# More landing places for the experts' value rows, in columns of the activations that are already used

## The chip, the cores and the metric

The kernel runs on one core of a Trainium2 chip. The metric is the device time of one execution in microseconds (us); the median of three runs stands for it.

## The reference, cut to what matters

One inference step of a two-layer decoder for 256 prompt tokens and 32 sample tokens (288 in all, width 1024). Each layer has an attention or state-space mixer and then a PEER channel mixer. In PEER, each token picks 16 experts for each of 8 heads out of 128 x 128 = 16384 experts:

```python
q = (xc @ w_q).reshape(P_CHUNK, P_HEADS, 2, P_DKEY // 2)
...
g = jax.nn.softmax(sc.astype(F32), axis=-1)
act = jax.nn.gelu(jnp.einsum('td,thkd->thk', xc, u_tab[eid]).astype(F32))
return jnp.einsum('thk,thkd->td', g * act, v_tab[eid].astype(F32)).astype(h.dtype)
```

So each token needs 128 rows of `v_tab`, each of 1024 float32 (4 KB), weighted by gate times activation and summed. For 288 tokens and two layers these are 576 sets of 128 rows, 512 KB each.

## The kernel before, in words

`peer(l)` stands once for each engine. TensorE first computes the activations of **all** experts for all tokens (`hidden`, lines 860 to 862): 128 steps, and ScalarE writes each step's result into `HID`, an SBUF region of four blocks (`HB[0]` to `HB[3]`, 9216 floats a partition each). A block is laid out column by column: 32 floats for each token, prompt tile 0 first (four tokens of a group side by side, `hidden_column`), then prompt tile 1, then the 32 sample tokens in columns 256 to 287.

Then comes the **value stage**, which the change touches. It goes over 72 groups of four tokens: 8 groups of sample tokens, then 32 groups of prompt tile 0, then 32 of prompt tile 1 (`GROUPS`, `NGR` = 72). TensorE's program is a loop over q (in `peer` of the tensor engine, after line 962), in a fixed order:

- `spread_i1(q)` (L889) copies the tokens' first expert indices over all partitions; VectorE makes a one-hot matrix of it (`one_hot`, L1974);
- `pick(q-1)` (L900) multiplies the one-hot matrix with the tokens' columns of `HID`: this is the last reading of these columns in this layer; it raises `picked_full`. VectorE then makes the weights (`weights`, L1981, L1988);
- `values(q-2)` (L918 for sample groups, L923 for prompt groups) multiplies the weights with the four tokens' gathered rows and adds up in PSUM; it waits for the four gathers and raises `v_used`.

The rows come by **gathers**: GpSimd issues one indirect DMA for each token (L639), 288 a layer, in the order of the groups, into `NVS` = 9 slots of 1024 floats (`VS`), used in turn. Gather n uses slot n modulo 9. The first nine wait for the end of the activations (`hidden_full` against `VS_FREE`), since these slots were buffers of that stage; each later one waits until the slot's former content is used: `v_used` >= (n - 9) // 4 + 1. GpSimd's program is in order, so a gather that waits holds up all later ones.

In layer 0 TensorE does work for the next layer inside the same loop: 64 key projections and 16 sets of sums (`key_norms`, L941 and L950), 20 steps in groups 29 to 38 and 60 steps in groups 43 to 71 (`NORM_PLACES`); VectorE and ScalarE do the state-space factors and the keys' squares beside it. These use parts of `HID` whose columns are picked already: pages of the latent cache land in `HB[2]` and `HB[3]` (SyncE loads them, L413, after 24 groups are picked), the factors, turns and key scales lie in `HB[0]` and `HB[1]`. Layer 1 has nothing beside its loop. After group 71 of layer 0 the odd layer begins; after group 71 of layer 1 the result is stored.

The lines that set the gathers' places and waits before:

```python
VS_FREE = [NK - 4 + n + 1 for n in range(4)] + [NK - 1, NK] + 3 * [NK]
...
if n < NVS:
    pool.wait_ge(sem("hidden_full"), l * NK + VS_FREE[n])
else:
    pool.wait_ge(sem("v_used"), l * NGR + (n - NVS) // 4 + 1)
```

Of the kernel before, what the change touches and what calls it, by code (L numbers as in the profile page):

```python
# [19 lines left out]
P = 128  # L20
D = 1024
# [3 lines left out]
NT = SEQ + NS  # L25
# [18 lines left out]
PH, TOPK, NK = 8, 16, 128  # L44
# [81 lines left out]
def build(nc, I, O, stop=4):  # L126
    ctx = ExitStack()
    with ctx:
# [140 lines left out]
        VS = [tile_at(f"v_slot{n}", [D], at) for n, at in enumerate(VS_AT)]  # L269
# [147 lines left out]
        def _(sp):  # L417
# [10 lines left out]
            load(ident, I["ident"], "ident_loaded")  # L428
            load(X[:, 1, :], I["x_prompt"][P:SEQ, :], "x_loaded1")
            load(gain, I["gain"], "gain_loaded")  # L430
# [3 lines left out]
            load(iota, I["iota"], "const_loaded")  # L434
            load(group, I["group"], "const_loaded")
            load(before, I["before"], "const_loaded")
            load(pages, I["page_table"], "pages_loaded")
            for n in range(1, 4):
                load(W_IN0[:, :, 512 * n:512 * n + 512], I["ev_w_in"][:, :, 512 * n:512 * n + 512], f"w_in0_loaded{n}")
            load(GAIN0, I["gain0"].partition_broadcast(P), "gain0_loaded")  # L440
            load(TBL0, I["tbl0"], "tbl0_loaded")
# [21 lines left out]
            load(TBLA, I["tbla"], "tbls_loaded")  # L463
            load(TBLB, I["tblb"], "tbls_loaded")
            load(TBLBN, I["tblbn"], "tbls_loaded")
# [17 lines left out]
            load(W_OUT, I["ev_w_out"], "w_out_loaded")  # L483
# [3 lines left out]
            def peer_loads(l):  # L487
# [17 lines left out]
                if l == 0 and live(3):  # L505

                    sp.wait_ge(sem("picked_full"), NS // 4)
                    load(S5P[:, 0:3, :], I["s5_par"], "s5_par_loaded")
                    load(BBD, I["s5_b"], "s5_b_loaded")
                    load(W_UKN, I["mla_w_uk"], "s5_b_loaded")  # L510
# [11 lines left out]
                    load(W_IN1, I["od_w_in"], "w_in1_loaded")  # L522
# [3 lines left out]
            if live(3):  # L526

                sp.wait_ge(sem("x_updated"), 2)
                load(GROW, I["grow"].partition_broadcast(P), "odd_small_loaded")
                load(GQN, I["mla_g_qn"].partition_broadcast(P), "odd_small_loaded")  # L530
                load(GQR, I["mla_g_qr"].partition_broadcast(P), "odd_small_loaded")
                load(GKN, I["mla_g_kn"].partition_broadcast(P), "odd_small_loaded")
                load(GKNP, I["mla_g_kn_col"], "odd_small_loaded")
                load(COS, I["cos"], "odd_small_loaded")
                load(SIN, I["sin"], "odd_small_loaded")
                load(W_UK, I["mla_w_uk"], "odd_small_loaded")
                load(W_UV, I["mla_w_uv"], "odd_small_loaded")
                load(W_UKT, I["mla_w_ukt"], "odd_small_loaded")
                load(W_GLU, I["s5_w_glu"], "odd_small_loaded")
                load(TBLD, I["tbld"], "odd_small_loaded")  # L540
                load(S0, I["state_c"], "odd_small_loaded")
                load(CBD, I["s5_c"], "odd_small_loaded")
                load(DSKIP, I["s5_d"], "odd_small_loaded")
                load(BGLU, I["s5_b_glu"], "odd_small_loaded")

                sp.wait_ge(sem("h_ready"), 18)
                load(W_UQ, I["mla_w_uq"], "w_uq_loaded")
# [13 lines left out]
                load(TBLDN, I["tbldn"], "tbldn_loaded")  # L561
# [19 lines left out]
                for n in range(2):  # L581
                    load(W_OUT1[n], I["od_w_out"][:, :, 512 * n:512 * n + 512], f"w_out1_loaded{n}")
# [20 lines left out]
        def _(pool):  # L603
# [14 lines left out]
            def peer(l):  # L618
# [11 lines left out]
                n = 0  # L630
                for g in GROUPS:
                    for t in group_tokens(g):
# [6 lines left out]
                        pool.indirect_dma_start(out=VS[n % NVS], out_offset=None, in_=v_rows,  # L639
                                                in_offset=bass.IndirectOffsetOnAxis(ap=IDX[:, at:at + 1], axis=0)).then_inc(sem(f"v_loaded{n % NVS}"), 16)  # L640
                        n += 1
# [27 lines left out]
        def _(pe):  # L669
# [90 lines left out]
            def out_projection(l, OT):  # L760
                pe.wait_ge(sem(f"ot_ready{l}"), 1)
                for n in range(2 if l else 1):
                    pe.wait_ge(sem(f"w_out1_loaded{n}" if l else "w_out_loaded"), 16)
# [32 lines left out]
            def peer(l):  # L796
# [106 lines left out]
                def values(q):  # L903
# [7 lines left out]
                    for i in range(4):  # L911
                        n = 4 * q + i
                        pe.wait_ge(sem(f"v_loaded{n % NVS}"), 16 * (l * (NT // NVS) + n // NVS + 1))
                    if kind == "sample":
                        for i in range(4):
                            w = WZ[:, 4 * (q % 4) + i, 31 - (4 * j + i):63 - (4 * j + i)]
                            for g in range(4):
                                ins = pe.matmul(banks[4][32 * g:32 * g + 32, 0:256], w, VS[(4 * q + i) % NVS][:, 256 * g:256 * g + 256],  # L918
                                                start=False, stop=False, skip_group_check=True)
# [1674 lines left out]
```

## Time and profile before

| what | us |
|---|---|
| median of 3 runs | 2413.12 (2412.98 to 2414.96) |
| span of the profiled execution, first to last instruction | 2379.3 |
| median less that span | 33.8 |
| gathers of layer 0, first to last issue | 730.5 to about 1168 |
| value groups 9 to 71 of layer 1 | 1989.8 to 2374.7 |
| TensorE busy in the whole span | 2003.3 (84%) |
| GpSimd busy in the whole span | 978.3 (41%) |

No time of its own is given for the profiled execution beyond its span; the 33.8 us between the span and the median lie around the span. In the profile, PE is TensorE, PEld its weight loads, DVE VectorE, ACT ScalarE, POOL GpSimd, SP SyncE; L639 is line 639. "PEclk" or "granted clock" is the share of TensorE's full clock. "DMA share" is the mean busy share of the core's 16 DMA engines; it adds up packet durations, so that overlapping packets can bring it a little over 1.

### The profile page before, as it was taken

The page shows a single profiled execution, that of the slowest core. Times are in us where ns is not written, and L with a number is a line of the kernel's source. Part 1 is how long each engine was busy: PE and PEld are TensorE (multiplying, and loading weights), DVE is VectorE, ACT ScalarE, POOL GpSimd, SP SyncE. Part 2 cuts the span into 40 slices and gives each one's busy share as a digit, 9 for nine tenths or more (in the row PEclk, how much of TensorE's full clock was granted, in tenths as well). Part 3 has the DMA queues.
Part 4 walks back from the last instruction along what each step waited for, and adds up shares of the span by engine and source line. Part 5 has one row for each costly group of instructions (what it writes and reads, how often), then busy time and mean ns, then how long its engine had stood idle before and what let it go on. Part 6 is the DMA issues. An engine that isn't in the chain of part 4 may idle for free.

```text
span 2379.3 us, 38222 instructions
## 1 busy us (share of the span) xinstructions
PE 2003.3 (84%) x14225; PEld 1500.4 (63%) x14225; DVE 1200.7 (50%) x3489; ACT 649.6 (27%) x977; POOL 978.3 (41%) x832
## 2 busy tenths in 40 slices
PE   9878999999998668889798478999999986666666
PEld 4554799999996333334366247999999963233322
DVE  2553499623333433588456944997233333333332
ACT  1331244555552001111124022455555520000000
POOL 0010368850003566666411303588500036655664
PEclk9898999999999789999887699999999998988887
DMA  6454424445457999999922334244545579998998
GB/s 231 188 208 160 151 90 160 160 160 166 163 168 242 345 338 379 373 369 354 344 72 64 88 110 151 86 159 159 165 162 167 165 249 335 357 354 321 349 337 311
DMA packets 176793, 529.89 MB, mean 223 GB/s; under 512 B 22018, under 2 KB 49186, under 8 KB 176098
## 3 DMA queue, kind: packets, MB, share of 16 engines
q0 software_dynamic: 86912, 309.64, 35.9%
q1 hardware_dynamic: 88546, 217.30, 27.0%
q8 instruction: 114, 1.87, 0.3%
q10 hardware_dynamic: 1152, 0.52, 0.1%
q14 instruction: 69, 0.57, 0.1%
HBM read 524.69 MB, written 2.69 MB: 222 GB/s over the span
## 4 chain that ended last, share of the span: by engine, by line
PE 58%; DMA 18%; POOL 9%; DVE 7%; issue 5%; ACT 2%; SPq 0%; POOLq 0%; DVEq 0%; ACTq 0%
DMA v_slot<-in_peer_v,v_rows 16%; PE bank L860 10%; PE bank L862 10%; PE bank L861 10%; PE bank L687 9%; PE bank L923 8%; POOL v_slot L639 6%; POOL u_low L627 3%; PE bank L1001 2%; PE bank L918 1%; PE bank L941 1%; DMA u_slot<-in_peer_ut 1%; PE bank L806 1%; PE bank L900 0%; DMA w_in<-in_od_w_in 0%
## 5 line engine op out<-in xcount | busy, mean ns | idle before, releaser
L639 POOL DMA_INDIRECT v_slot<-in_peer_v,v_rows x576 | 544.7, 946 | 771.5 <-PE bank L862 441.1
L860 PE MATMUL bank<-h_parts,u_high 128*128 128x288 f32 x2048 | 607.0, 296 | 7.4 <-POOL u_low L627 5.8
L861 PE MATMUL bank<-h_parts,u_high 128*128 128x288 f32 x2048 | 604.4, 295 | 0.0
L862 PE MATMUL bank<-h_parts,u_low 128*128 128x288 f32 x2048 | 602.8, 294 | 0.0
L923 PE MATMUL bank<-v_slot,weight_columns 128*32 128x512 f32 x2048 | 304.9, 720 | 208.6 <-DMA v_slot<-in_peer_v,v_rows 205.7
L860 PEld LDWEIGHTS bank<-h_parts,u_high 128*128 128x128 f32 x2048 | 384.1, 188 | 11.2 <-POOL u_low L627 9.2
L862 PEld LDWEIGHTS bank<-h_parts,u_low 128*128 128x128 f32 x2048 | 385.7, 188 | 0.0
L861 PEld LDWEIGHTS bank<-h_parts,u_high 128*128 128x128 f32 x2048 | 384.6, 188 | 0.0
L1429 ACT CAST u_high<-u_slot 128x1024 fp32r<-128x1024 f32 x256 | 268.8, 1050 | 400.1 <-PE bank L862 244.2
L627 POOL TENSOR_TENSOR u_low<-u_slot,u_high 128x1024 fp32r<-128x1024 f32 x120 | 319.2, 2670 | 95.0 <-ACT u_high L1429 95.0
L1961 DVE TENSOR_TENSOR u_low<-u_slot,u_high 128x1024 fp32r<-128x1024 f32 x136 | 166.7, 1226 | 277.7 <-ACT u_high L1429 277.7
L1974 DVE TENSOR_SCALAR i_one_hot<-bank,keep 128x512 f32<-128x512 f32 x144 | 108.0, 751 | 383.9 <-PE bank L889 377.0
L923 PEld LDWEIGHTS bank<-v_slot,weight_columns 128*32 128x32 f32 x2048 | 69.0, 121 | 346.2 <-issue 300.4
L1981 DVE SCALAR_TENSOR_TENSOR i_one_hot<-keep,i_pairs,bank 128x128 f32<-128x128 f32 x576 | 165.7, 344 | 58.3 <-PE bank L900 58.0
L1459 ACT ACTIVATE hidden_rows<-bank 128x288 f32<-128x288 f32 x256 | 180.9, 707 | 10.4 <-PE bank L862 10.3
L900 PE MATMUL bank<-hidden_rows,i_one_hot 128*128 128x128 f32 x1152 | 174.4, 299 | 3.4 <-DVE i_one_hot L1974 3.4
L900 PEld LDWEIGHTS bank<-hidden_rows,i_one_hot 128*128 128x128 f32 x1152 | 158.4, 210 | 26.0 <-issue 15.8
L622 POOL TENSOR_TENSOR w_q_low<-w_q,w_q_high 128x1024 fp32r<-128x1024 f32 x24 | 57.2, 2393 | 198.8 <-ACT w_q_high L1439 198.8
L889 PEld LDWEIGHTS bank<-i_tokens,keep 128*128 128x128 bf16 x576 | 37.0, 105 | 139.7 <-issue 137.8
L1525 ACT ACTIVATE key_squared<-bank 128x512 f32<-128x512 f32 x64 | 38.2, 597 | 295.7 <-PE bank L941 295.7
L413 POOL DMA_DIRECT2D region<-in_pool_kv x32 | 17.4, 543 | 173.6 <-issue 173.6
L687 PE MATMUL bank<-h_parts,w_q_high 128*128 128x288 f32 x384 | 77.9, 298 | 0.0
(368 smaller groups left out, 2297.9 us busy)
## 6 DMA issues: line engine op xcount, KB each, us to landing
u_slot<-in_peer_ut SPq DMA_DIRECT2D x256, 512.0 KB, 3.5
w_q<-in_peer_w_q SPq DMA_DIRECT2D x8, 2048.0 KB, 17.4
v_slot<-in_peer_v,v_rows POOLq DMA_INDIRECT x576, 6.2
region<-in_cache_a_kt SPq DMA_DIRECT2D x8, 960.0 KB, 11.3
region<-in_cache_a_v SPq DMA_DIRECT2D x8, 960.0 KB, 12.7
region<-in_ev_w_in SPq DMA_DIRECT2D x3, 2048.0 KB, 15.6
region<-in_pool_kv POOLq DMA_DIRECT2D x32, 128.0 KB, 3.3
region<-in_pool_kv SPq DMA_DIRECT2D x32, 128.0 KB, 3.3
```

The source lines that it names most:

```text
L627: pool.tensor_tensor(ULOW[e % 4], US[e % 4], UHIGH[high_slot(e)].bitcast(F32), ALU.subtract).then_inc(sem("u_split_by_pool"), 1)
L639: pool.indirect_dma_start(out=VS[n % NVS], out_offset=None, in_=v_rows, in_offset=bass.IndirectOffsetOnAxis(ap=IDX[:, at:at + 1], axis=0)) ...
L687: ins = pe.matmul(out, lhsT, rhs, start=(n == 0), stop=(n == len(pairs) - 1))
L860: pe.matmul(bank, uh, HR[:, 0, c, :], start=(c == 0), stop=False)
L861: pe.matmul(bank, uh, HR[:, 1, c, :], start=False, stop=False)
L862: ins = pe.matmul(bank, ul, HR[:, 0, c, :], start=False, stop=(c == KC - 1))
L900: ins = pe.matmul(out, OH1[:, q % 2, i, :], HID[:, :, hidden_column(t), :], start=True, stop=True)
L923: ins = pe.matmul(banks[6 - 2 * kind + h][32 * i:32 * i + 32, :], WZ[:, 4 * (q % 4) + i, 31 - j:63 - j], VS[(4 * q + i) % NVS][:, 512 * h: ...
L1429: act.copy(UHIGH[high_slot(e)], US[e % 4]).then_inc(sem("u_high"), 1)
L1459: act.activation(HID[:, e // ROWS, :, e % ROWS], banks[4 + e % 4][:, 0:NT], ACT.Gelu_apprx_tanh).then_inc(sem("gelu_done"), 1)
L1961: dve.tensor_tensor(ULOW[e % 4], US[e % 4], UHIGH[high_slot(e)].bitcast(F32), ALU.subtract).then_inc(sem("u_split_by_dve"), 1)
L1981: step(dve.scalar_tensor_tensor(out=OH1[:, q % 2, i, :], in0=iota, scalar=I2T[:, t:t + 1], in1=banks[2 + q % 2][:, i * P:i * P + P], op0=A ...
```

## The change

Layer 0 gets nine and layer 1 eight further slots of 1024 floats, in columns of `HID` that have been picked. A table, worked out when the program is built, gives each gather its slot, the semaphore and count it waits for, and how many landings its slot has had by then. A slot stands in the table with the place in the loop at which it comes free (16.3: right after the picking in pass 16 of the loop), and is taken by the gather that comes next; after use by group g it comes free at g + 2.7. In layer 0 the slots that the side work needs later have a last group (34, 37 or 47) after which they are not used.

```diff
+def value_plan(places, landings):
+    spare, plan = list(places), []
+    for n in range(NT):
+        place = min(p for p in spare if n // 4 <= p[4])
+        spare.remove(place)
+        _, slot, signal, count, last = place
+        landings[slot] += 1
+        plan.append((slot, signal, count, landings[slot]))
+        spare.append((n // 4 + 2.7, slot, "v_used", n // 4 + 1, last))
+    return plan
...
-        VS = [tile_at(f"v_slot{n}", [D], at) for n, at in enumerate(VS_AT)]
+        V_FIRST = [(n - NVS, at, "hidden_full", count, NGR) for n, (at, count) in enumerate(zip(VS_AT, VS_FREE))]
+        V_COLUMNS = ([(12.0, HB[0] + 8192, "s5_factors_made", 2, 34)]
+                     + [(16.3 + 8 * m, HB[0] + D * m, "picked_full", 16 + 8 * m, 37) for m in range(3)]
+                     + [(16.3 + 8 * m, HB[1] + D * m, "picked_full", 16 + 8 * m, 47) for m in (2, 3)]
+                     + [(16.3 + 8 * m, HB[k] + D * m, "picked_full", 16 + 8 * m, NGR) for m, k in ((4, 0), (4, 1), (5, 0))],
+                     [(8.3, HB[k] + 8192, "picked_full", 8, NGR) for k in range(4)]
+                     + [(16.3, HB[k], "picked_full", 16, NGR) for k in range(4)])
...
-                        if n < NVS:
-                            pool.wait_ge(sem("hidden_full"), l * NK + VS_FREE[n])
-                        else:
-                            pool.wait_ge(sem("v_used"), l * NGR + (n - NVS) // 4 + 1)
-                        at = hidden_column(t)
-                        pool.indirect_dma_start(out=VS[n % NVS], ...
+                for t, (slot, signal, count, _) in zip(tokens, V_PLAN[l]):
+                    pool.wait_ge(sem(signal), before_layer[signal] + count)
+                    at = hidden_column(t)
+                    pool.indirect_dma_start(out=VS[l][slot], ...
...
-                        pe.wait_ge(sem(f"v_loaded{n % NVS}"), 16 * (l * (NT // NVS) + n // NVS + 1))
+                    for slot, _, _, landing in V_PLAN[l][4 * q:4 * q + 4]:
+                        pe.wait_ge(sem(f"v_loaded{slot}"), 16 * landing)
```

By this table layer 0 has 9 slots up to group 12, then 10, from group 16 on 11, from 24 on 12, from 33 on 14, after 34 again 13, after 37 only 10, from 40 on 11, after 47 first 9 and then 11, from 56 on 12. Layer 1 has 9 up to group 8, then 13, from group 17 on 17.

Each slot has a semaphore, so nine more are needed. The rest of the diff makes room for them: loads that come at different times share one semaphore with added-up counts (`ident_loaded` and `w_in1_loaded` become `ident_then_w_in1_loaded`, `w_out_loaded` joins `w_in0_loaded3`, and so on), and the waits' counts follow. The loads themselves, their order and their queue stay.

## Rows read from the trace of the kernel before

**Rows 1.** Page: the span, and the span in 40 slices of 59.5 us.
```profile
span 2379.3 us, 38222 instructions
...
PEclk9898999999999789999887699999999998988887
...
GB/s 231 188 208 160 151 90 160 160 160 166 163 168 242 345 338 379 373 369 354 344 72 64 88 110 151 86 159 159 165 162 167 165 249 335 357 354 321 349 337 311
```

**Rows 2.** The tile `v_slot`, whole span: durations in ns, min/median/max.
```profile
L639 POOL DMA_INDIRECT v_slot<-in_peer_v,v_rows x576: 932/937/1884, 730.5 to 2366.5; - x192
...
DMA to landing us min/median/max: 4.2/6.2/9.0
```

**Rows 3.** Windows for `v_slot` alone: length, PE, PEld, POOL busy, PEclk, DMA share, GB/s.
```profile
1989.82:2374.70 384.88, 158.53 (x1008) 35.45 (x1008) 231.27 (x247) 0.85 0.94 342
824.52:926.74 102.22, 41.13 (x256) 8.95 (x256) 60.14 (x65) 0.82 0.98 353
926.74:1002.05 75.31, 27.76 (x208) 6.62 (x208) 48.70 (x52) 0.95 1.00 376
1002.05:1149.63 147.58, 48.02 (x400) 11.68 (x400) 97.60 (x100) 1.00 0.98 364
1149.63:1179.07 29.44, 13.02 (x80) 2.81 (x80) 14.47 (x15) 0.83 0.93 338
```

**Rows 4.** The chain that ended last, layer 1: start, us, what.
```profile
2103.53 0.93 POOL v_slot L639
...
2106.01 5.76 DMA v_slot<-in_peer_v,v_rows
...
2111.90 3.31 PE bank L923 x16
...
2115.47 0.94 POOL v_slot L639
```

**Rows 5.** Waits in 1990 to 2374: us in total, times, longest.
```profile
PE bank L923 <- DMA v_slot<-in_peer_v,v_rows: 130.5, 59, 5.5
POOL v_slot L639 <- PE bank L923: 85.6, 46, 5.2
```

**Rows 6.** Windows, all instructions: length; PE, PEld, DVE, ACT, POOL; PEclk, DMA, GB/s.
```profile
2132.00:2134.00 2.00, 1.05 (x10) 0.86 (x8) 1.66 (x8) 0.00 (x0) 1.39 (x3) 1.00 0.95 299
...
2138.00:2140.00 2.00, 2.00 (x12) 0.22 (x4) 0.00 (x0) 0.00 (x0) 0.00 (x0) 0.50 1.02 416
...
2110.00:2116.00 6.00, 4.10 (x26) 1.57 (x27) 1.01 (x6) 0.00 (x0) 3.05 (x4) 0.72 1.02 385
2047.00:2070.00 23.00, 12.85 (x116) 6.69 (x119) 8.31 (x40) 0.00 (x0) 15.86 (x18) 1.00 1.01 392
...
975.00:981.00 6.00, 4.68 (x28) 1.83 (x29) 2.00 (x11) 0.00 (x0) 2.63 (x3) 0.75 1.04 394
...
963.00:969.00 6.00, 5.18 (x42) 2.35 (x46) 2.29 (x12) 2.45 (x3) 3.97 (x5) 1.00 1.02 410
```

**Rows 7.** PE in order of time, layer 1, at full and at half clock.
```profile
2048.31 1.93 PE L923 MATMUL bank<-v_slot,weight_columns 128*32 128x512 f32 x16 [3.31 <-DMA v_slot<-in_peer_v,v_rows]
...
2050.40 1.11 PE L900 MATMUL bank<-hidden_rows,i_one_hot 128*128 128x128 f32 x8
...
2087.37 3.59 PE L923 MATMUL bank<-v_slot,weight_columns 128*32 128x512 f32 x16 [1.87 <-DMA v_slot<-in_peer_v,v_rows]
```

**Rows 8.** DMA issues between 880 and 925: the key pages in layer 0.
```profile
ckv_t_norm<-in_pool_ckv SPq DMA_DIRECT2D x32, 64.0 KB
```

**Rows 9.** Windows, all instructions (columns as in Rows 6): groups 42 to 66, layer 0.
```profile
1002.05:1149.63 147.58, 133.72 (x890) 58.32 (x891) 113.01 (x450) 28.50 (x48) 97.60 (x100) 1.00 0.98 364
```

**Rows 10.** VectorE and GpSimd in order of time, around group 12 of layer 0.
```profile
811.91 0.69 DVE L1677 TENSOR_TENSOR s_b_scaled<-s_b_tmp 128x512 f32<-128x512 f32 x1
...
813.72 0.93 POOL L639 DMA_INDIRECT v_slot<-in_peer_v,v_rows  x1 [0.30 <-issue]
```

More of the change, by code:

```diff
@@ L268, in build @@
         VS_FREE = [NK - 4 + n + 1 for n in range(4)] + [NK - 1, NK] + 3 * [NK]
-        VS = [tile_at(f"v_slot{n}", [D], at) for n, at in enumerate(VS_AT)]
+        V_FIRST = [(n - NVS, at, "hidden_full", count, NGR) for n, (at, count) in enumerate(zip(VS_AT, VS_FREE))]
[5 more added lines that the diff above has]
+                     + [(16.3, HB[k], "picked_full", 16, NGR) for k in range(4)])
+        V_PLAN, landings = [], [0] * (NVS + 9)
+        for columns in V_COLUMNS:
+            places = V_FIRST + columns
+            V_PLAN.append(value_plan([(when, slot, signal, count, last) for slot, (when, _, signal, count, last) in enumerate(places)], landings))
+        VS = [[tile_at(f"v_slot{n}" if n < NVS else f"v_slot_of_columns{l}{n}", [D], at) for n, (_, at, *_) in enumerate(V_FIRST + V_COLUMNS[l])]
+              for l in range(2)]
         OH1 = tile_at("i1_one_hot", [2, 4, P], HR_AT)
@@ L544, in _ @@
[L544 removed]
+                load(GROW, I["grow"].partition_broadcast(P), "tbls_then_odd_small_loaded")
+                load(GQN, I["mla_g_qn"].partition_broadcast(P), "tbls_then_odd_small_loaded")
+                load(GQR, I["mla_g_qr"].partition_broadcast(P), "tbls_then_odd_small_loaded")
+                load(GKN, I["mla_g_kn"].partition_broadcast(P), "tbls_then_odd_small_loaded")
+                load(GKNP, I["mla_g_kn_col"], "tbls_then_odd_small_loaded")
@@ new lines, in _ @@
+                load(COS, I["cos"], "tbls_then_odd_small_loaded")
+                load(SIN, I["sin"], "tbls_then_odd_small_loaded")
+                load(W_UK, I["mla_w_uk"], "tbls_then_odd_small_loaded")
+                load(W_UV, I["mla_w_uv"], "tbls_then_odd_small_loaded")
+                load(W_UKT, I["mla_w_ukt"], "tbls_then_odd_small_loaded")
+                load(W_GLU, I["s5_w_glu"], "tbls_then_odd_small_loaded")
+                load(TBLD, I["tbld"], "tbls_then_odd_small_loaded")
+                load(S0, I["state_c"], "tbls_then_odd_small_loaded")
@@ L629, in peer @@
                 pool.wait_ge(sem("rows_ready"), l + 1)
-                n = 0
-                for g in GROUPS:
-                    for t in group_tokens(g):
-                        if n < NVS:
-                            pool.wait_ge(sem("hidden_full"), l * NK + VS_FREE[n])
-                        else:
-                            pool.wait_ge(sem("v_used"), l * NGR + (n - NVS) // 4 + 1)
-                        at = hidden_column(t)
-                        pool.indirect_dma_start(out=VS[n % NVS], out_offset=None, in_=v_rows,
-                                                in_offset=bass.IndirectOffsetOnAxis(ap=IDX[:, at:at + 1], axis=0)).then_inc(sem(f"v_loaded{n % NVS}"), 16)
-                        n += 1
+                before_layer = {"hidden_full": l * NK, "picked_full": l * NGR, "v_used": l * NGR, "s5_factors_made": 0}
+                tokens = [t for g in GROUPS for t in group_tokens(g)]
+                for t, (slot, signal, count, _) in zip(tokens, V_PLAN[l]):
+                    pool.wait_ge(sem(signal), before_layer[signal] + count)
+                    at = hidden_column(t)
+                    pool.indirect_dma_start(out=VS[l][slot], out_offset=None, in_=v_rows,
+                                            in_offset=bass.IndirectOffsetOnAxis(ap=IDX[:, at:at + 1], axis=0)).then_inc(sem(f"v_loaded{slot}"), 16)
             if live(2):
@@ L910, in values @@
                     pe.wait_ge(sem("weights_ready"), l * NGR + q + 1)
-                    for i in range(4):
-                        n = 4 * q + i
-                        pe.wait_ge(sem(f"v_loaded{n % NVS}"), 16 * (l * (NT // NVS) + n // NVS + 1))
+                    slots = []
+                    for slot, _, _, landing in V_PLAN[l][4 * q:4 * q + 4]:
+                        pe.wait_ge(sem(f"v_loaded{slot}"), 16 * landing)
+                        slots.append(VS[l][slot])
                     if kind == "sample":
@@ L917, in values @@
                             for g in range(4):
-                                ins = pe.matmul(banks[4][32 * g:32 * g + 32, 0:256], w, VS[(4 * q + i) % NVS][:, 256 * g:256 * g + 256],
+                                ins = pe.matmul(banks[4][32 * g:32 * g + 32, 0:256], w, slots[i][:, 256 * g:256 * g + 256],
                                                 start=False, stop=False, skip_group_check=True)
@@ L923, in values @@
                                 ins = pe.matmul(banks[6 - 2 * kind + h][32 * i:32 * i + 32, :], WZ[:, 4 * (q % 4) + i, 31 - j:63 - j],
-                                                VS[(4 * q + i) % NVS][:, 512 * h:512 * h + 512], start=False, stop=False, skip_group_check=True)
+                                                slots[i][:, 512 * h:512 * h + 512], start=False, stop=False, skip_group_check=True)
                     ins.then_inc(sem("v_used"), 1)
@@ L1512, in _ @@
                 peer(0)
-            act.wait_ge(sem("s5_par_loaded"), 16)
+            act.wait_ge(sem("gain0_then_s5_par_loaded"), 32)
             act.activation(S5P[:, 3, :], S5P[:, 2, :], ACT.Exp).then_inc(sem("s5_mag"), 1)
@@ L1553, in odd @@
                     copy_out(BT[:, k, :, :].rearrange("p a b -> p (a b)"), full()[:, :], "s5_bt_ready")
-                act.wait_ge(sem("odd_small_loaded"), 16 * 16)
+                act.wait_ge(sem("tbls_then_odd_small_loaded"), 48 + 16 * 16)
                 for t, rows, a in TILES:
```

88 lines of the change are left out of this document (38 added, 50 removed).

## The prediction

> **What bounds the kernel now.** I looked first at the slices of the page: in slices 12 to 19 and 32 to 39, the value stages of the two layers, the core moves 242 to 379 GB/s, elsewhere at most 231 [rows 1]. Then at the tile `v_slot`: 576 gathers, issued in 0.94 us each, landing 6.2 us after issue in the median, 4.2 at the least [rows 2]. Then at the windows from the end of one group's value products to the end of another's; the count of matmuls checks the groups, 16 for each [rows 3]. Layer 1, groups 9 to 71: 63 groups in 384.88 us, **6.11 us for a group**, 1.527 for a gather. Layer 0: groups 13 to 28 in 102.22 us (6.39 each), 29 to 41 in 75.31 (5.79), 42 to 66 in 147.58 (5.90), 67 to 71 in 29.44 (5.89).
>
> What sets the 6.11 us? A share of 0.94 for the DMA engines looks like a full pipe, but the chain tells a loop [rows 4]: the products free a slot, POOL issues three gathers 1.24 us apart (2103.53 to 2106.01), the last lands after 5.76, the products take 3.31, and POOL begins again at 2115.47: 11.9 us, and that for two groups, since with nine slots a gather's slot comes from two or three groups before. Both sides wait in turns: PE 130.5 us for landings, POOL 85.6 us for PE [rows 5]. So layer 1 is bound by the **latency of a loop over nine slots**. Within it the rate swings: 299 GB/s soon after a pause of POOL, 416 once the queue has filled (the first two of [rows 6]). In the one stretch where the pauses happened to be short and even, 2047 to 2070, it is 392 GB/s at a share of 1.01; 385 in 2110 to 2116; in layer 0 394 in 975 to 981 and 410 in 963 to 969 [rows 6].
>
> **The change part by part.** What is added is depth; no gather, byte or matmul is removed.
>
> Layer 1. From group 8 on four more slots, from 17 on eight. With 13 or 17 the last gather of a group takes its slot from three or more groups back, so the loop of 12 us is spread over at least three groups: at most 4 us for a group, no longer the bound. What is late next is the largest of three. POOL: 1.24 us for a gather [rows 4], 4.96 for a group. TensorE at full clock: from the start of one group's value products (2048.31) over the spread to the end of the pick (2050.40 + 1.11) 3.2 us for a group [rows 7]. DMA: I take 390 GB/s, the middle of 385, 392 and 394 [rows 6], so 524,288 B in 1.344 us, **5.38 us for a group**. The DMA engines bind. 63 groups take 338.9 us, 46 less than 384.88; I take off 1 for the queue to fill: **45 us**. Bounds of this rate: above, the 1.24 us of POOL's issue; below, packets that stay as long as they now are on average: 342 GB/s at a share of 0.94, so 364 GB/s at 1.0 [rows 3], 1.44 us, 5.76 for a group. I take the middle, since the long stretch with even issue lies there.
>
> The Trainium skill speaks against that rate: "DMA: Bandwidth & Descriptors", Specifications, limits HBM for one core to about 358 GB/s. By that page a gather would take an estimated 1.464 us and a group 5.86, and the whole change would bring some 19 us in place of 64. The trace disagrees: 392 GB/s stood for 23 us here [rows 6].
>
> Layer 0. The same rate, with two differences. First, the slots come late and some go again: 10 from group 12, 11 from 16, up to 14. With 10, only the last two gathers of a group wait for the group two before it, one issue less in the loop: (11.9 - 1.24) / 2 = 5.3 us, so even 10 slots come to about the DMA's pace. Second, SyncE's key pages share the engines: 32 issues of 64 KB in 880 to 925 [rows 8], 2.1 MB or 5.4 us at 390 GB/s, and two later sets of half that, 2.7 us each.
> - Groups 13 to 28: 16 x 5.38 + 5.4 = 91.5 against 102.22, 10.7 less; 9, since four of them have only 10 slots.
> - 29 to 41: 13 x 5.38 + 2.7 = 72.6 against 75.31: 2.7.
> - 42 to 66: DMA alone 25 x 5.38 + 2.7 = 137.2 against 147.58. But TensorE is busy for 133.72 of it and VectorE for 113.01, at full clock [rows 9]: two streams nearly full that also wait for each other. I take half of the 10.4: 5.
> - 67 to 71: 29.44 - 5 x 5.38 = 2.5.
> Sum for layer 0: **19 us** (between 6 by 5.76 us for a group and about 35 by 5.12, the 410 GB/s of [rows 6]).
>
> Edits with no cost. POOL's and PE's waits are as many as before, on other counts. The new signals stand in POOL's queue, and all later gathers are behind them. `picked_full` comes before the `v_used` that a gather would otherwise want, by the fixed order of TensorE's loop. `s5_factors_made` 2, for the second gather of group 12, is ready at 812.6, while that gather was issued at 813.72 anyway [rows 10]; the cover is 1.1 us, and without it the gathers behind would move by what is missing, with six or more gathers' worth of landings under way. The shared semaphores add up loads whose earlier part has long landed when the later is waited for. SyncE's queue keeps its order; its key pages are used four or more groups after their issue, and at a pace of 5.4 instead of 6.4 us that is still 20 us for 5.4 us of transfer. What comes before the value stages and after them only moves earlier.
>
> Sum: 45 + 19 = 64 us of the span of 2379.3. The 33.8 us by which the median exceeds the span stay, so 2413.1 - 64 = **2349 us**.
>
> **The rivals.** (1) *The long packets stay.* If the slow packets belong to the transfers or to POOL's issuing and not to the shallow queue, the share can only rise to 1.0: 5.76 us for a group. Layer 1 gives 384.88 - 362.9 = 22, layer 0 6: 2385 us. For it: layer 0 from 42 to 66 has a share of 0.98 and only 364 GB/s [rows 3]. Against: 392 GB/s over 23 us with POOL issuing throughout [rows 6]. The limit of 358 GB/s in the Trainium skill ("DMA: Bandwidth & Descriptors", Specifications) would act the same way; an estimate by it is 2394.
>
> (2) *Only layer 1 gains.* In layer 0 the pages, TensorE and VectorE take what the depth gives: 2413 - 45 = 2368. For it: 133.72 of 147.58 us busy [rows 9]. Against: groups 13 to 28 have none of that work and are the slowest, 6.39 us.
>
> (3) *The rate goes on rising with depth,* up to POOL's 4.96 us for a group: 72 in layer 1, and about 35 in layer 0, where TensorE's side work caps it: 2306. For it: 416 and 410 GB/s in short windows. Against: no window over 6 us has it.
>
> (4) *TensorE falls to half clock and binds: slower.* The clock is at 1.00 in the even stretch and at 0.85 over the groups 9 to 71 [rows 3, 6]: it goes to half (1.2 GHz) for pieces between full ones (2.4 GHz). At half, the value products took 3.59 us instead of 1.93 [rows 7], and a whole group would take 2 x 3.2 = 6.4. If it stayed there, 63 x (6.4 - 6.11) = 18 us more: 2431. It decides from a mean clock under 3.2 / 6.11 = 0.52. Against: the even pace kept the clock full (2047 to 2070), and deeper prefetch makes the pace even.
>
> (5) *Nothing happens:* the share of 0.94 to 1.00 is the true limit and the pauses only look like one, or the table's slots come free too late to be issued ahead: 2413.
>
> **How the numbers follow.** Forecast 0.55, (1) 0.20, (2) 0.08, (3) 0.07, (4) 0.06, (5) 0.04. A measurement of this kernel can tell about 0.2%, 5 us, from no change (its three runs span 2 us). The first four are faster: 0.90; same 0.04; slower 0.06. For the range I go from the rate of 410 GB/s in both layers (5.12 us: 62 + 35 less, 2316) to the lowest that the rows allow: 353 GB/s at a share of 0.98 in groups 13 to 28 [rows 3] is 360 at 1.0, 5.83 us for a group, 18 + 3 less, 2392. That leaves out (4), (5) and most of (3), under 0.2.
>
> **What would show it.** Right: in layer 1 the 63 groups take about 339 us at a DMA share of 1.0 or more and 385 to 395 GB/s; a gather lands 12 us or more after its issue, not 6, because it queues; PE still waits for landings, 1.5 to 2 us in each group; POOL waits for PE with a full queue behind it; clock above 0.85; groups 13 to 28 of layer 0 take about 93 us. Rival (1) shows as 360 GB/s at a share of 1.0; (2) as unchanged windows in layer 0; (3) as POOL without waits for PE; (4) as a clock near 0.5 and value products of 3.6 us throughout. The forecast is wrong if the time before or after the value stages moves, or if the gathers still land after 6 us while POOL pauses.

## The result and the profile after

| | median us | runs |
|---|---|---|
| before | 2413.05 | 4 (2411.94 to 2414.96) |
| changed kernel | 2389.36 | 4 (2383.30 to 2394.38) |

The ratio is 0.9896 with an interval of 0.9872 to 0.9921: **24 us faster** (1.0%), where 64 (2.7%) were forecast. It lies inside the range of 2316 to 2392, near its upper end. All ratios below are of runs in each chip's usual state; one run of the changed kernel in batch 3, 2582.9 us long at a granted clock of 0.73, is not in them.

One thing has to be set right before the two profiles are compared. The profiled run of the changed kernel took 2384.45 us for a span of 2382.8, so only 1.65 us lie around a span, and this holds for each of its runs. The 33.8 us "around the span" of the kernel before were no such thing: its profiled execution took some 2381 us, 32 less than each of its timed runs. It came from another chip, as will be seen. A profile of before on a chip like that of the times was therefore needed; it is the first experiment below, and its rows are called **before, second profile**.

The changed kernel's page, all of it in 40 slices as in [rows 1] (granted clock, DMA share, GB/s; the value stages are slices 12 to 19 and 33 to 39):

```profile
span 2382.8 us, 38222 instructions
...
PEclk9798999999999888999898679999999999879888
DMA  6455424444456999999941234144454469999998
GB/s 231 175 192 189 150 79 155 158 165 163 167 167 227 346 356 371 351 327 341 337 163 55 75 124 160 55 158 152 162 166 167 162 199 350 362 344 351 368 355 320
```

Windows from group to group, as in [rows 3] and [rows 9] but for all instructions (length; PE, PEld, DVE, ACT, POOL busy; PEclk, DMA share, GB/s): groups 13 to 28, 29 to 41, 42 to 66 and 67 to 71 of layer 0, then 9 to 71 of layer 1. First the changed kernel, on the chip of the comparison:

```profile
829.94:932.39 102.45, 71.36 (x458) 33.98 (x458) 32.43 (x160) 2.39 (x4) 62.85 (x68) 0.80 0.98 360
932.39:1010.08 77.69, 66.29 (x429) 28.49 (x429) 32.66 (x144) 10.27 (x16) 46.88 (x51) 0.91 0.97 357
1010.08:1173.86 163.78, 143.38 (x891) 61.84 (x890) 114.46 (x455) 28.50 (x48) 100.03 (x102) 0.94 0.94 333
1173.86:1199.58 25.72, 20.16 (x140) 9.17 (x140) 16.53 (x61) 3.12 (x7) 11.24 (x12) 0.87 0.99 368
2006.67:2378.15 371.48, 276.73 (x1753) 112.56 (x1752) 129.16 (x633) 0.00 (x0) 230.84 (x247) 0.87 0.96 353
```

Then before, second profile. It is from the chip of batch 1 below, where the kernel before takes 2405.87 us in the median, 7 less than on the chip of the comparison:

```profile
831.18:933.95 102.77, 65.54 (x457) 30.71 (x458) 32.97 (x160) 2.39 (x4) 61.20 (x66) 0.87 0.97 348
933.95:1014.74 80.79, 63.99 (x430) 28.58 (x429) 35.36 (x159) 10.28 (x16) 48.87 (x52) 0.94 0.98 358
1014.74:1165.70 150.96, 134.30 (x890) 58.55 (x891) 113.17 (x449) 28.52 (x48) 97.96 (x100) 1.00 0.97 355
1165.70:1197.73 32.03, 23.64 (x140) 10.64 (x140) 15.38 (x52) 3.12 (x7) 14.09 (x15) 0.73 0.94 343
2007.75:2401.09 393.34, 256.42 (x1752) 120.43 (x1752) 128.21 (x621) 0.00 (x0) 232.17 (x247) 0.84 0.93 335
```

So layer 1 went from 393.3 to 371.5 us, 5.90 us for a group, 22 us less: nearly the whole gain. Layer 0 gained nothing: 0.3 and 3.1 us less in the first two windows, 12.8 more in the third, 6.3 less in the last, 3.1 more in the sum.

Who waits for what in layer 1 has changed. The changed kernel's waits between 2006.67 and 2378.15 (us in total, times, longest):

```profile
DVE i_one_hot L1997 <- remote: 140.6, 46, 10.1
...
POOL v_slot L662 <- remote: 58.1, 27, 2.9
DVE i_one_hot L2004 <- PE bank L922: 52.3, 24, 4.2
...
PE bank L946 <- DVE weight_columns L2011: 29.4, 14, 2.4
...
PE bank L946 <- DMA v_slot<-in_peer_v,v_rows: 7.7, 3, 2.9
```

And one line of before, second profile:

```profile
PE bank L923 <- DMA v_slot<-in_peer_v,v_rows: 117.4, 48, 4.5
```

TensorE waited 117.4 us for landings there (130.5 in the first profile, [rows 5]) and now 7.7: the rows are there in time. What decides now is when TensorE's signals come. VectorE's one-hot waits for such a signal, and the profile calls the releaser "remote". The signal is on record each time, but more than 1.5 us after the recorded end of any matmul that raises it, so the profile does not connect the two. Four rows of the timeline show it, with the spread of `i_tokens` (PE L911), the one-hot that waits for it (DVE L1997) and the weights that free the value products (L2011, L946):

```profile
2236.07 0.40 PE L911 MATMUL bank<-i_tokens,keep 128*128 128x128 bf16 x4
...
2240.11 0.17 DVE L2011 TENSOR_TENSOR weight_columns<-picked,gate_pairs 128x4 f32<-128x4 f32 x1
...
2240.33 1.06 PE L946 MATMUL bank<-v_slot_of_columns,weight_columns 128*32 128x512 f32 x1 [2.62 <-issue]
...
2243.37 0.75 DVE L1997 TENSOR_SCALAR i_one_hot<-bank,keep 128x512 f32<-128x512 f32 x1 [3.10 <-remote]
```

The last spread matmul ends at 2236.47, VectorE has been idle for 3.10 us, and still the one-hot starts at 2243.37. The trace's record of the signals says where the 6.9 us go: the spread's signal comes at 2243.34, and the one-hot starts 0.03 us later. The signals of the value products before it (recorded end 2236.1) and of the pick after it (2237.7) come with it, all between 2243.28 and 2243.43. VectorE's own signals are prompt: the 184 of layer 1 that can be matched to an instruction come 0.01 us after its end, and the value products start 0.05 us after their weights are written.

Over the 72 groups of layer 1 the one-hot starts 3.3 us after the recorded end of the spread in the median and over 6.6 in one of four; in the first profile of before it is 0.04 us in nine of ten. In nine of ten groups it starts 0.03 us after the signal, so the time lies between the recorded end of TensorE's work and its signal, not in VectorE. I call this a **late signal**. A matmul's end is modelled in the profile, so the record does not tell whether the matmuls end later than shown or only their signals come late. Outside the two value stages TensorE's signals are prompt in the same trace: all 425 that can be matched to a matmul come within 0.04 us of its recorded end. Inside them, while the gathers run, they come up to 13 us after it.

### The profile page after: what moved, and what is told of

Its sections match the earlier page's. It is cut to its first block, busy times and chain, and to the rows that moved or that the text cites. A ratio compares the mean times of both kernels' runs of the same rounds, so it can differ in the third digit from the quotient of the medians.

```text
span 2382.8 us, 38222 instructions
## 1 busy us (share of the span) xinstructions
PE 2039.0 (86%) x14225; PEld 1493.2 (63%) x14225; DVE 1195.8 (50%) x3489; ACT 649.7 (27%) x977; POOL 979.5 (41%) x832
## 4 chain that ended last, share of the span: by engine, by line
PE 66%; DVE 9%; another core or an unknown queue 8%; issue 6%; POOL 5%; DMA 3%; ACT 2%; SPq 2%; DVEq 0%; POOLq 0%; ACTq 0%
PE bank L882 10%; PE bank L884 10%; PE bank L883 10%; PE bank L946 8%; PE bank L709 8%; PE bank L922 4%; POOL u_low L653 3%; PE bank L964 3%; PE bank L1024 2%; DVE i_one_hot L2004 1%; PE bank L911 1%; DMA v_slot<-in_peer_v,v_rows 1%; POOL v_slot L662 1%; PE bank L941 1%
## 5 line engine op out<-in xcount | busy, mean ns | idle before, releaser
L662 POOL DMA_INDIRECT v_slot<-in_peer_v,v_rows x417 | 394.3, 946 | 720.5 <-PE bank L884 441.1
L946 PE MATMUL bank<-v_slot,weight_columns 128*32 128x512 f32 x1412 | 270.8, 677 | 47.3 <-DMA v_slot<-in_peer_v,v_rows 25.7
L946 PE MATMUL bank<-v_slot_of_columns,weight_columns 128*32 128x512 f32 x636 | 251.5, 698 | 68.6 <-issue 32.7
L1997 DVE TENSOR_SCALAR i_one_hot<-bank,keep 128x512 f32<-128x512 f32 x144 | 107.9, 751 | 335.7 <-remote 216.5
L662 POOL DMA_INDIRECT v_slot_of_columns<-in_peer_v,v_rows x159 | 150.7, 948 | 52.6 <-issue 47.3
L946 PEld LDWEIGHTS bank<-v_slot,weight_columns 128*32 128x32 f32 x1412 | 53.2, 116 | 143.3 <-issue 137.7
L946 PEld LDWEIGHTS bank<-v_slot_of_columns,weight_columns 128*32 128x32 f32 x636 | 43.0, 116 | 150.4 <-issue 113.6
```

The costliest lines, as they stand in the source:

```text
L662: pool.indirect_dma_start(out=VS[l][slot], out_offset=None, in_=v_rows, in_offset=bass.IndirectOffsetOnAxis(ap=IDX[:, at:at + 1], axis=0)) ...
L946: ins = pe.matmul(banks[6 - 2 * kind + h][32 * i:32 * i + 32, :], WZ[:, 4 * (q % 4) + i, 31 - j:63 - j], slots[i][:, 512 * h:512 * h + 512 ...
```

## Experiments

All ran on one of five chips, batch by batch; kernels of a batch share the chip and the runs of before. "Layer 1" below is the length of its groups 9 to 71, from windows like those above. Each edit is against the changed kernel, or where it says so, against *layer 1 alone*.

**Batch 1: before 2405.87 us (23 runs).** Parts of the change.

The kernel before, unchanged.

> The kernel before, unchanged, to read a second profile of it. Theory A (the first profile of before was of an execution some 32 us faster than all timed ones: its span is 2379.3 us and the other runs of both kernels lie 1.65 us around their span): this profile's span is 2410 to 2413 us, and the groups of four tokens of layer 1's value loop take more than the 6.11 us of the first profile, about 6.4 us. Theory B (some 34 us lie around the span of before, as the prediction assumed): the span is 2379 us again and a group 6.11 us.

Time 2407.39, span 2405.7. Theory A holds: the first profile of before is of a faster chip. A group takes 6.24 us in layer 1. The signals are late here too, but less: the one-hot starts 0.5 us after the spread's recorded end in the median.

Layer 1 alone:

```diff
-        V_COLUMNS = ([(12.0, HB[0] + 8192, "s5_factors_made", 2, 34)]
...
+        V_COLUMNS = ([],
```

> Additional slots in layer 1 alone. If most of the change's 24 us comes from layer 1 (the two traces give a group of 6.11 before and 5.90 after, 13 us in all, and layer 0 gave nothing): 2395 to 2400 us against 2413 for before. If layer 0's slots cost time, as its groups 42 to 66 (147.6 us before, 163.8 after) suggest: below the changed kernel's 2389, about 2375. If the traces mislead and the gain is in layer 0: 2410.

2381.60 us, 0.9886 (0.9866 to 0.9906), layer 1 in 367.9. Layer 1's slots are worth 24 us here, as much as the whole change on the chip of the comparison. The one-hot now starts 3.1 us late in the median, on the same chip that has 0.5 with nine slots.

Layer 0 alone:

```diff
-                     [(8.3, HB[k] + 8192, "picked_full", 8, NGR) for k in range(4)]
-                     + [(16.3, HB[k], "picked_full", 16, NGR) for k in range(4)])
+                     [])
```

> Additional slots in layer 0 alone. By the traces (groups 13 to 71 of layer 0 took 354.5 us before and 369.7 us after): slower than before by up to 15 us, 2413 to 2428. By the prediction's sum (19 us in layer 0): 2394. If the second profile of before shows a slower loop than the first: between the two, 2400.

2403.09 us, 0.9978 (0.9959 to 0.9997): 3 us, where 19 were forecast. Its groups 42 to 66 of layer 0 take 160.3 us against 151.0 of before on this chip, and the changed kernel 157.1 on batch 5's chip, so the slower window of the comparison (163.8) was no accident of one run; groups 67 to 71 win back 5.4.

No additional slots:

```diff
-        V_COLUMNS = ([(12.0, HB[0] + 8192, "s5_factors_made", 2, 34)]
...
+        V_COLUMNS = ([], [])
```

> The changed kernel with both lists of additional places empty: nine slots as before, and only the merged semaphores and the written-out plan remain. If merging semaphores is without effect: 2413, the same as before, and in the profile the value products' signal follows their recorded end by 0.03 us. If the merged semaphores delay TensorE's signals (in the changed kernel's trace they come 0 to 8 us after the recorded end): slower than before, 2420 or more.

2406.07 us, 0.9989 (0.9973 to 1.0004). Merged semaphores and the written-out plan cost nothing that can be measured. They are not what makes signals late: with them and nine slots the one-hot starts 0.6 us late in the median, before has 0.5, and layer 1 alone, with the same semaphores and more slots, 3.1.

**Batch 2: before 2386.16 us (11 runs).** What binds layer 1 with more slots. All four against layer 1 alone.

Half the bytes, as many issues:

```diff
-                    pool.indirect_dma_start(out=VS[l][slot], out_offset=None, in_=v_rows,
+                    halves = I["peer_v"].rearrange("l a b (h d) -> (l a b h) d", h=2)
+                    pool.indirect_dma_start(out=VS[l][slot][:, 0:D // 2] if l else VS[l][slot], out_offset=None, in_=halves if l else v_rows,
...
```

> Slots of layer 1 alone, and in layer 1 each gather brings rows of 2 KB in place of 4 KB (the right half of each value row is left out, and its products read the left half again): as many issues, half the bytes. Reference for it: slots of layer 1 alone, 0.9886 of before, layer 1's groups 8 to 71 in 368 us. Theory D (the loop is bound by the DMA engines' rate): the groups fall from 5.84 us to the next bound, POOL's four issues of 1.24 us = 4.96, 313 us for the 63 groups, 0.966 of before. Theory H (it is bound by the hand-offs between TensorE and VectorE, whose signals come late): 368 us still, 0.989.

Half the products:

```diff
-                        for h in range(2):
+                        for h in range(1 if l else 2):
```

> Slots of layer 1 alone, and in layer 1's prompt groups only the four value products of the left half are computed (the products of the right half are left out): about 1.0 us less of TensorE's work in each group at full clock. Theory D: the same as with all products, 368 us for the groups, 0.989 of before, within 3 us. Theory H: up to 1 us less a group, 305 to 340 us, 0.96 to 0.975 of before.

Thirteen slots:

```diff
-                     + [(16.3, HB[k], "picked_full", 16, NGR) for k in range(4)])
+                     )
```

> Layer 1's eight additional slots cut to the four that open at group 8: thirteen slots in all. Theory D: thirteen do what seventeen do, groups 8 to 71 in 368 to 371 us, 0.989 of before. If depth still counts (a loop over the slots of a fixed latency, as with nine): between nine and seventeen, 378 to 385 us, 0.993 to 0.996.

Plain loads by SP under the same waits, on semaphores of their own:

```diff
...
+                    for n, (slot, signal, count, _) in enumerate(V_PLAN[l]):
+                        sp.wait_ge(sem(signal), before_layer[signal] + count)
+                        load(VS[l][slot], v_rows[NK * NK + 128 * (n % 100):NK * NK + 128 * (n % 100) + P, :], plain_loaded(slot)[0])
...
```

> Slots of layer 1 alone, and in layer 1 each gather is replaced by a plain load of the same 512 KB, 128 consecutive rows, issued by SP under the same waits; POOL issues nothing there. What is left out: the picking of the rows by index. In the trace of the reference the gathers move 349 GB/s while POOL is issuing (packets of 179 ns in the mean) and 407 GB/s more than 1.3 us after an issue (163 ns). Theory D with the issuing as the cause of the slow packets: 400 to 410 GB/s, a group in 5.15 us, groups 8 to 71 in 325 us, 0.971 of before. Theory D with another cause: 368 us, 0.989. Theory H: 368 us with the DMA engines idle for a tenth of the time.

| kernel | median us | ratio | layer 1, us | GB/s, DMA share |
|---|---|---|---|---|
| half the bytes | 2307.24 | 0.9659 (0.9626 to 0.9691) | 316.9 | 210, 0.73 |
| half the products | 2324.45 | 0.9733 (0.9699 to 0.9768) | 329.2 | 401, 1.01 |
| thirteen slots | 2321.98 | 0.9732 (0.9702 to 0.9762) | 330.4 | 399, 1.00 |
| plain loads | 2318.99 | 0.9715 (0.9676 to 0.9753) | 326.1 | 403, 1.01 |

I had expected 368 us as the reference, from batch 1, and here thirteen slots alone gave 330: 64 us less than before, not 24. Either the chip or the number of slots made the difference; batch 3 was to tell. Within this batch three kernels agree at some 5.2 us for a group and 400 GB/s, with all the products or half of them, with gathers or plain loads. So POOL's issuing costs the DMA engines nothing that shows here, against the reading of the slow packets in the last expectation; and with half the bytes a group takes 5.03 us, POOL's 4.96 [rows 4]. Here the DMA engines bind, with POOL 3% behind.

**Batch 3: before 2388.43 us (11 runs).** Chip or slots.

The changed kernel.

> The changed kernel itself again, with the three others of this batch on one chip. So far two chips: on the first (before 2406 us) seventeen slots in layer 1 gave 368 us for groups 8 to 71 with 4% of the packets over 300 ns; on the second (before 2386 us) thirteen gave 330 us with 0.2%. Theory C (the chip decides: on one kind the gathers' packets stay long and TensorE's signals come late, on the other neither): on a chip of the first kind 0.99 of before, on one of the second 0.97 (2315 to 2325 us). Theory S (seventeen slots do worse than thirteen): 0.99 on either.

Layer 1 alone, seventeen slots.

> Seventeen slots in layer 1 alone, on the same chip as the changed kernel. Theory C: equal to thirteen slots on this chip within 3 us: 0.989 of before on a chip of the first kind, 0.973 on the second. Theory S: 0.989, and thirteen 0.973, on one chip. Its distance to the changed kernel is what layer 0's slots bring: 0 to 5 us by the first chip's pair.

Thirteen slots in layer 1 alone.

> Thirteen slots in layer 1 alone. Theory C: as seventeen, 0.973 on a chip like the second (packets over 300 ns 0.2%, 409 GB/s) or 0.989 on one like the first. Theory S: 0.973 whatever the chip.

The kernel before.

> The kernel before, for its profile on this chip. Theory C: on a chip of the second kind its groups 8 to 71 of layer 1 take 385 us as in the first profile of before (span 2379), with 4 to 5% of the packets over 300 ns all the same, since nine slots let the queues run empty; on a chip of the first kind 393 us.

| kernel | median us | ratio | layer 1, us |
|---|---|---|---|
| changed kernel | 2297.08 | **0.9623** (0.9586 to 0.9660) | 330.0 |
| seventeen in layer 1 | 2328.41 | 0.9761 (0.9726 to 0.9795) | 327.9 |
| thirteen in layer 1 | 2325.84 | 0.9745 (0.9715 to 0.9775) | 330.4 |
| before | 2386.23 | one run | 384.8 |

The chip decides (theory C). The same changed kernel gains 91 us here: 60 by layer 1's slots, 31 more by layer 0's. Against layer 1 alone on this chip, layer 0's windows are 11.7, 3.8, 8.5 and 7.8 us shorter. The changed kernel's windows, in the order of those above:

```profile
830.64:919.96 89.32, 62.36 (x460) 30.36 (x459) 33.22 (x160) 2.39 (x4) 61.92 (x66) 0.90 1.03 396
919.96:991.37 71.41, 62.39 (x429) 28.23 (x429) 35.70 (x159) 10.28 (x16) 47.91 (x52) 0.95 1.04 401
991.37:1131.95 140.58, 133.14 (x889) 57.24 (x890) 112.39 (x449) 28.53 (x48) 98.39 (x101) 1.00 1.00 388
1131.95:1155.14 23.19, 17.61 (x141) 8.39 (x140) 15.47 (x52) 3.11 (x7) 11.27 (x12) 0.93 0.97 375
1961.14:2291.18 330.04, 224.70 (x1753) 106.83 (x1752) 129.45 (x621) 0.00 (x0) 230.97 (x246) 0.93 1.00 399
```

and its GB/s in 40 slices:

```profile
GB/s 239 158 199 219 154 49 157 154 164 160 166 165 165 326 382 396 401 399 393 379 166 52 62 109 133 94 150 156 166 161 164 165 167 288 409 409 409 410 408 330
```

409 GB/s in five slices of layer 1. The signals are prompt, and TensorE waits for landings, 105 us in all; three of the waits in layer 1, and then two rows around a spread:

```profile
DVE i_one_hot L1997 <- PE bank L911: 170.9, 60, 4.5
...
PE bank L946 <- DMA v_slot<-in_peer_v,v_rows: 82.2, 46, 3.1
...
PE bank L946 <- DMA v_slot_of_columns<-in_peer_v,v_rows: 23.2, 16, 1.9
```

```profile
2128.55 0.40 PE L911 MATMUL bank<-i_tokens,keep 128*128 128x128 bf16 x4
...
2128.98 0.75 DVE L1997 TENSOR_SCALAR i_one_hot<-bank,keep 128x512 f32<-128x512 f32 x1 [1.88 <-PE bank L911]
```

From the last spread to the one-hot it is a few hundredths of a microsecond; in the rows of the other chip above it was 6.9. A gather lands 13.2 to 13.8 us after its issue in the median, by slots. The packets tell the same. I counted gathers issued but not landed, as a mean over the DMA engines, in the middle of layer 1: 2.0 to 2.1 with nine slots on either kind of chip, with 4 to 5% of the packets over 300 ns; 7.0 with the changed kernel here, with 0.1%. On batch 1's chip seventeen slots left it at 2.3 and 3.4% long: the slots were there, but the signals that free them came late, and the queue stayed nearly as shallow as with nine.

**Batch 4: before 2386.45 us (9 runs).** Was it a latency loop, and the two controls again, all against layer 1 alone.

Eleven slots in layer 1:

```diff
-                     [(8.3, HB[k] + 8192, "picked_full", 8, NGR) for k in range(4)]
-                     + [(16.3, HB[k], "picked_full", 16, NGR) for k in range(4)])
+                     [(8.3, HB[k] + 8192, "picked_full", 8, NGR) for k in range(2)])
```

> Layer 1's additional slots cut to two: eleven in all. On a chip where thirteen slots give 330 us for groups 8 to 71 and nine give 385: the latency theory of the prediction has 9 slots for 6.11 us a group, so 11 slots give 5.0 us, under the DMA engines' 5.13, and so 325 to 335 us, 0.975 of before. If the gain grows with the depth in equal steps instead: half way, 357 us, 0.987. On a chip with late signals: 380 to 393 us, 0.99 to 1.0.

2325.64 us, 0.9736 (0.9709 to 0.9762), layer 1 in 326.7. **Two more slots do all that eight do**, on chips with prompt signals; eleven were not tried on one with late signals. A latency of 9 / 4 x 6.11 = 13.7 us over eleven slots is 5.0 us for a group, under the DMA engines' 2,097,152 B at 409 GB/s, 5.13. That is the loop of the prediction.

Half the bytes and half the products:

> Seventeen slots in layer 1 alone, rows of 2 KB in place of 4 KB there (the right half of each value row is left out). On a chip with late signals, theory D (the DMA engines bind): groups 8 to 71 in 313 to 320 us, POOL's issues. Theory H (the hand-offs bind): 360 to 370 us, as with whole rows. On a chip without: 317 us as before.

> Seventeen slots in layer 1 alone, half the value products in its prompt groups (the products of the right half are left out). On a chip with late signals, theory D: 368 us for groups 8 to 71, 0.989 of before. Theory H: less by up to 1 us a group, 305 to 350 us, 0.965 to 0.98. On a chip without: 0.973 as before, DMA-bound at 409 GB/s.

The chip had no late signals, so they only repeat batch 2: 0.9652 (0.9621 to 0.9684) and 0.9732 (0.9700 to 0.9764).

**Batch 5: before 2407.56 us (11 runs).** This one fell on a chip with late signals.

The changed kernel.

> The changed kernel on one more chip. On a chip with late signals 0.985 to 0.992 of before (2385 to 2395 us against 2405 to 2415); on one without 0.962 (2297 against 2388).

2382.74 us, 0.9881 (0.9855 to 0.9907); the comparison's result again.

Half the bytes, half the products, with layer 1's slots alone. Their reference on this chip is the changed kernel, which has the same slots in layer 1; layer 1 alone was not run here:

> Seventeen slots in layer 1 alone, rows of 2 KB in place of 4 KB there. On a chip with late signals, theory D (the DMA engines bind): groups 8 to 71 of layer 1 in 313 to 320 us. Theory H (the hand-offs bind): 360 to 370 us. On a chip without: 317 us, 0.965 of before.

> Seventeen slots in layer 1 alone, half the value products in its prompt groups. On a chip with late signals, theory D: 368 us for the groups, 0.989 of before. Theory H: 305 to 350 us, 0.965 to 0.98. On a chip without: 0.973.

0.9865 (0.9837 to 0.9894) and 0.9855 (0.9828 to 0.9882). Layer 1's groups 9 to 71 of the three (changed kernel, half the bytes, half the products), each from its own windows:

```profile
1997.70:2365.60 367.90, 275.09 (x1752) 112.08 (x1750) 129.16 (x633) 0.00 (x0) 231.60 (x247) 0.88 0.96 357
```

```profile
2009.00:2372.20 363.20, 280.35 (x1756) 109.35 (x1752) 126.57 (x621) 0.00 (x0) 230.59 (x244) 0.92 0.62 180
```

```profile
2011.20:2376.70 365.50, 212.47 (x1248) 116.59 (x1248) 128.92 (x635) 0.00 (x0) 231.84 (x248) 0.72 0.97 361
```

With half the bytes the engines are busy for 0.62 of the time, and 4.7 us are gained of 368. With half the products TensorE is busy for 212 us in place of 275, and 2.4 are gained. So on such a chip **neither the DMA engines nor TensorE's recorded work binds**. POOL does not either: its 231 us of issues are the same as on the prompt chip, where with half the bytes they allow 316.9. What is left are the hand-offs from TensorE to VectorE and POOL, whose signals the trace shows late: 142.3 us of VectorE's waits in the second kernel are again "remote", and the one-hot starts 2.6 us late in the median, 4.6 in the third kernel:

```profile
DVE i_one_hot L1995 <- remote: 142.3, 50, 10.1
```

The share of 0.96 and the 357 GB/s of the changed kernel look like a full pipe, and are none: take half the bytes away, and the time stays. The half products came out as theory D said (368), the half bytes as theory H (360 to 370). Theory D falls by the bytes; of theory H the part falls by which less work for TensorE would shorten the loop (305 to 350 us).

## Why the prediction was right and wrong

- *The latency loop over nine slots*: right. Eleven slots remove it where nothing else is late, and the full rate appears at once.
- *The DMA engines bind at 390 GB/s, 5.38 us for a group*: right in kind on the chips with prompt signals, and 5% too slow: they reach 409 GB/s, and layer 1 took 330.0 us where 338.9 were forecast (384.8 less 330.0 is 55, against 45). The 5.38 us of the sum measured 5.24. The 392 GB/s of [rows 6] were still a queue that now and then ran low; 410 GB/s, the bound I left to the range, was the rate.
- *"The DMA engines bind"* is **the step that failed** on the chip of the comparison, with the sentence behind it that what is late next is the largest of three (POOL, TensorE at full clock, DMA). The fourth was not in the sum: the chain spread, one-hot, pick, weights, products, in which TensorE's signals come 3.3 us late in the median there. The sum's 3.2 us for TensorE are rows of the first profile, in which the one-hot follows the spread by 0.04 us. On chips with late signals a group stays at 5.77 to 5.90 us whatever the bytes or products. Layer 1 gave 22 us of 45.
- *Layer 0's 19 us*: on the chip of the comparison nothing, and batch 1 gives 3 us for it alone. Groups 42 to 66, with over 5 us of TensorE's work in each (134.3 in 25 groups) and hand-offs to ScalarE besides, went the wrong way: 163.8 us against 151.0, and 160.3 with layer 0's slots alone. That it is the late signals there too is argued, not tested. On the chip of batch 3 it is 31 us: 89.3, 71.4, 140.6 and 23.2 against 102.2, 75.3, 147.6 and 29.4 [rows 3], so 12.9, 3.9, 7.0 and 6.2 for the forecast 10.7 (taken as 9), 2.7, 5 and 2.5. Each stage moved the way that was forecast and by more, the last 2.5 times as much.
- *The 33.8 us around the span stay*: wrong in kind. They were the difference of two chips. I took 45 + 19 us worked out on a profile with prompt signals from a median of a chip with late ones; a profile some 1.3% faster than every timed run should have been a warning, and a rival ("the profile is not of the timed chip") belonged in the text.
- *Rivals (2) and (3)*: on chips with late signals layer 0 gained next to nothing, as (2) had it, but layer 1 gave half of what (2) takes for it. On the chips with prompt signals 409 GB/s stood for five slices, against "no window over 6 us has it" in (3); POOL's 4.96 us became the bound only with half the bytes.
- *Rival (1), long packets stay, 2385 us*: the number nearest to 2389, and for another reason. They stay where the queue stays shallow. That it is not the packets that bind there is shown by the half rows.
- *The limit of 358 GB/s*: 409 GB/s over five slices of 57 us go against it. The Trainium skill says elsewhere ("Perfetto Trace Analysis", Engine Utilization, Roofline) that 358 GB/s is the share of a core when both of a pair use the memory, and that a core alone can reach about 120% of it; an estimate by that is 430 GB/s. By that, the trace agrees, at 114%.
- *Rival (4), TensorE at half clock*: did not decide. The mean clock in layer 1 was 0.87, and with half the products 0.72, at the same time.
- *What would show it*: "PE still waits for landings, 1.5 to 2 us in each group" came true on the chips with prompt signals (105 us in layer 1, 1.7 a group) and false on the others (7.7). On the former a gather lands 13 to 14 us after its issue, where 12 or more were forecast; on the latter the landing records are too few to tell. "POOL waits for PE with a full queue behind it" held only in part: POOL waits for PE for 15 us in layer 1 of the changed kernel on batch 3's chip. TensorE's missing waits for landings did tell which step had failed.

What stays open is what makes the signals late. It depends on the chip: the comparison's and those of batches 1 and 5 have it, with before at 2406 to 2413 us; those of batches 2 to 4 and of the first profile of before do not, at 2381 to 2388. On such a chip it also depends on the kernel: 0.5 us with nine slots and 3.1 with seventeen, both on batch 1's. The traces of these chips also lack records: of the 4,608 landing signals of layer 1 (16 for each of 288 gathers) batch 1's chip holds 2,825 with nine slots and 1,875 with seventeen, the changed kernel on the comparison's chip 1,848, and on batch 3's chip 4,592. The Trainium skill ("NOTIFIC — the notification-queue block", 7.1) says that the block which writes such records can stall the engine that feeds it when its internal buffers are full. No run here shows whether that is the cause, or whether missing records and late signals have a common one; no experiment without the profiler was made.

## What to carry to other kernels

Where transfers bind, a slot count beyond what covers the latency buys nothing: latency over the time for one transfer at the full rate gives the number, and here two more slots were enough for layer 1 on the chips with prompt signals. Before a forecast, compare the profiled span with the timed runs; if they differ by more than what lies around a span, they may be of different chips, and what binds may differ too. A DMA share near 1 shows no bound by itself: halve the bytes and see.

## What the runs showed of the hardware that was not expected

- Chips differ in what a kernel gains: the same change is worth 1.0, 1.2 and 3.8% on three of them, while the kernel before differs by only 1%. With nine slots TensorE's signals are late by 0.5 us in the median on a chip where they are late by 3.1 with seventeen, so a profile of the kernel before shows little of it.
- The late signals are TensorE's and come only while the gathers run: VectorE's come 0.01 us after the end of its instruction at the same time, and outside the value stages TensorE's come within 0.04 us.
- 128 rows of 4 KB each are gathered at 409 GB/s once the queue holds three gathers or more. With two, 4% of the packets take over 300 ns (median 159) and the mean rises from 163 to 179 ns: packets of the same size take longer though less is moved, so a packet's duration holds waiting. With eleven slots (3.0 gathers in flight) only 0.4% are long.
- Gathers by index on POOL and plain loads of the same size by SP move the same 400 GB/s and give the same time (330.4 and 326.1 us).
